# A hybrid decoder block with 15 Strassen pairs instead of 12, eight projection units per head turn, two score buffers, and a softmax division shared by two engines

## The reference, cut to what matters

```python
D_MODEL = 1024; SEQ = 1024; HEAD_DIM = 64; N_Q_HEADS = 16; N_KV_HEADS = 4; WINDOW = BLOCK = 128; CONV_K = 3; D_FF = 2816

proj = jnp.einsum('bsd,de->bse', x, w_in[l])                       # float32, 1024 x 1024 by 1024 x 6656
q, k, v, cb, cc, ch, g_conv, g_attn = jnp.split(proj, SPLIT_POINTS, axis=-1)
y_conv = cb * causal_depthwise_conv(cc * ch, conv_w[l])            # width 3
# sliding-window attention by blocks of 128 queries against their own and the previous 128 keys
scores = where(valid, einsum('bnqkgd,bnskd->bnkgqs', qb, kb) * HEAD_DIM ** -0.5 + alibi, NEG_INF)
m = maximum(max(scores), sink)
p = exp(scores - m)
probs = p / (sum(p) + exp(sink - m))
y_attn = einsum('bnkgqs,bnskd->bnqkgd', probs, vb)
merged = sigmoid(g_conv) * y_conv + sigmoid(g_attn) * y_attn
x = layer_norm(ALPHA * x + einsum('bse,ed->bsd', merged, w_out[l]), ln1_g[l], ln1_b[l])
hid = silu(x @ w_gate[l]) * (x @ w_up[l])
x = layer_norm(ALPHA * x + hid @ w_down[l], ln2_g[l], ln2_b[l])
```

## Time and profile before

| | |
|---|---|
| median of 3 runs | 1359.15 us (1354.24 to 1359.17) |
| the profiled execution's own time | 1358.13 us |
| its span, first to last instruction | 1356.3 us |
| TensorE busy | 1340.0 us, 99% |
| VectorE busy | 848.1 us, 63% |
| ScalarE busy | 528.0 us, 39% |
| GpSimd busy | 724.8 us, 53% |
| mean granted TensorE clock | 0.996 |

### The profile page before, as it was taken

How to read it: one execution, slowest core, us unless ns; L and a number is a source line. 1 busy time by engine, 2 the same in 40 slices (tenths; PEclk the granted TensorE clock), 3 DMA queues, 4 the chain that set the end, 5 groups by cost and what they waited for, 6 DMA issues and landing times. The chain is left out here.

```text
span 1356.3 us, 18062 instructions
## 1 busy us (share of the span) xinstructions
PE 1340.0 (99%) x6506; PEld 1176.5 (87%) x6506; DVE 848.1 (63%) x1167; ACT 528.0 (39%) x973; POOL 724.8 (53%) x487
## 2 busy tenths in 40 slices
PE   9999999999999999999899999999999999999997
PEld 8888888888888888888788888888888888888886
DVE  5665555576867778787968754545546455464547
ACT  6422322336565565755345332232322313223143
POOL 5588788721222121336682775563756637566374
PEclk9999999999999999999999999999999999999999
DMA  6111222121111111112330221211212112111113
GB/s 187 48 55 55 62 63 63 51 59 48 32 34 45 47 32 32 47 48 78 109 93 1 70 71 47 71 54 39 70 46 70 53 40 70 46 59 58 47 55 125
DMA packets 128816, 80.58 MB, mean 59 GB/s; under 512 B 8816, under 2 KB 123504, under 8 KB 128752
## 3 DMA queue, kind: packets, MB, share of 16 engines
q1 hardware_dynamic: 128752, 79.73, 19.8%
HBM read 75.53 MB, written 4.19 MB: 59 GB/s over the span
## 5 line engine op out<-in xcount | busy, mean ns | idle before, releaser
L828 POOL TENSOR_TENSOR w_lo<-raw,w_hi 128x512 fp32r<-128x512 f32 x80 | 110.3, 1379 | 204.0 <-ACT w_hi L1201 204.0
L679 POOL TENSOR_TENSOR w_lo<-raw,w_hi 128x1024 fp32r<-128x1024 f32 x28 | 68.5, 2447 | 219.9 <-ACT w_hi L887 209.9
L1664 DVE TENSOR_TENSOR res<-res,ps 128x512 f32<-128x512 f32 x128 | 87.2, 687 | 59.8 <-PE ps L1835 59.8
L1833 PE MATMUL ps<-hid_hi,wd_hi 128*128 128x512 f32 x320 | 121.5, 380 | 0.1
L1834 PE MATMUL ps<-hid_lo,wd_hi 128*128 128x512 f32 x320 | 121.3, 379 | 0.0
L1835 PE MATMUL ps<-hid_hi,wd_lo 128*128 128x512 f32 x320 | 121.3, 379 | 0.0
L2127 PE MATMUL ps<-act_hi,w_hi 128*128 128x512 f32 x320 | 121.3, 379 | 0.0
L2128 PE MATMUL ps<-act_lo,w_hi 128*128 128x512 f32 x320 | 121.3, 379 | 0.0
L2129 PE MATMUL ps<-act_hi,w_lo 128*128 128x512 f32 x320 | 121.3, 379 | 0.0
L1833 PE MATMUL ps<-act_hi,w_hi 128*128 128x512 f32 x272 | 104.5, 384 | 0.0
L1834 PE MATMUL ps<-act_lo,w_hi 128*128 128x512 f32 x272 | 103.1, 379 | 0.0
(11 more groups left out here) (262 smaller groups left out, 3590.1 us busy)
## 6 DMA issues: line engine op xcount, KB each, us to landing
raw<-in_w_in SPq DMA_DIRECT2D x28, 512.0 KB, 3.8
raw<-in_w_in SPq DMA_DIRECT2D x48, 256.0 KB, 3.0
raw<-in_w_gate SPq DMA_DIRECT2D x40, 256.0 KB, 2.8
raw<-in_w_up SPq DMA_DIRECT2D x40, 256.0 KB, 3.2
raw_d<-in_w_down SPq DMA_DIRECT2D x20, 512.0 KB, 3.4
raw<-in_w_out SPq DMA_DIRECT2D x16, 512.0 KB, 4.0
xs<-in_x SPq DMA_DIRECT2D x8, 512.0 KB, 6.9
out<-rows SPq DMA_DIRECT2D x7, 512.0 KB, 2.7
```

Source lines behind the costliest of these rows:

```text
L828: pool.tensor_tensor(wide(ring(w_lo, n)), src, fp(wide(ring(w_hi, n))), ALU.subtract).then_inc(pl_s, 1)
L1664: dve.tensor_tensor(tile, tile, bank, ALU.add).then_inc(add_s, 1)
L1833: pe.matmul(bank, w_h(t), hi, start=(t == 0), stop=False)
```

## The change

`PLAIN` becomes `(3,)`. Three more (gc, cb) pairs are made ahead of the heads (15 in all), and the turns of the first three heads have 8 units and 8 steps per block; the fourth keeps 12. Consequences in the code:

- The places of the attention's actions in short turns are new. The fourth head's are the same but for the added division.
- There are two score buffers, `sc` and `sc_even`, taken in turn. The exponentials are written back into the same buffer, one column to the left; `exps` is gone. The sink column is written twice per head (prep_dve counts 9 per head instead of 8).
- VectorE multiplies two of the four query heads' probabilities, ScalarE the other two (`divide`, a Copy with the reciprocal as its scale). The transposes wait for both.
- In the fourth turn the ga units are in another order and the weight slots change over (`head_slot`, `before_in_slot`).
- In the first pair GpSimd makes the third weight sum one step earlier. In the output projection's second half the sums x = high + low of token half 1 are spread among the later units instead of standing in one row, and the mean, variance and spread of token half 0 are made earlier on TensorE.

```diff
-PLAIN = (0, 1, 2, 3)
+PLAIN = (3,)
...
-    UNITS += [(_i, 0), (_i + 1, 0), (_i, 1), (_i + 1, 1)]
+    UNITS += [(_i, 0), (_i + 1, 0)] + ([(_i + 1, 1), (_i, 1)] if _k in PLAIN else [(_i, 1), (_i + 1, 1)])
...
-PE_STEPS = sorted([(block_at(b, 0), "scores", b) for b in BLOCKS] + [(block_at(b, 14, 11), "turn", b) for b in BLOCKS]
-                  + [(block_at(b, 20, 15), "values", b) for b in BLOCKS])
+PE_STEPS = sorted([(block_at(b, 0), "scores", b) for b in BLOCKS] + [(block_at(b, 14, 12.5), "turn", b) for b in BLOCKS]
+                  + [(block_at(b, 20, 20.4), "values", b) for b in BLOCKS])
...
+    [(block_at(b, 8.4, 7.7), "divide", b) for b in BLOCKS],
...
-    [(block_at(b, 22.2, 17.2), "values", b) for b in BLOCKS],
+    [(block_at(b, 22.2, 25.5), "values", b) for b in BLOCKS],
...
-    [(LAST_TURN + 113.2 + 0.1 * (m - 6), "mix_second", m) for m in (6, 7)],
+    [(LAST_TURN + 112 + 0.1 * (m - 6), "mix_second", m) for m in (6, 7)],
     [(out_end(DT - 2) + 0.4, "x_second", 0)],
-    [(out_end(DT - 1) + 0.4 + 0.1 * m, "x_second", m) for m in range(1, DT)])
+    [(out_end(DT - 1) + 0.4 + 0.1 * m, "x_second", m) for m in range(1, 3)])
...
-                    act.activation(prob_and_sink(g, lo), sc[:, g, lo:], ACT.Exp, bias=neg_m[:, g:g + 1], scale=-1.0,
+                    act.activation(sc_of(b)[:, g, lo:2 * P + 1], scores_and_sink(b, lo)[:, g], ACT.Exp, bias=neg_m[:, g:g + 1], scale=-1.0,
                                    accum_out=rsum[:, g:g + 1]).then_inc(exp_s, 1)
+
+            def divide(b):
+
+                lo = P if b % NB == 0 else 0
+                act.wait_ge(soft_s, SOFT * b + 3)
+                for g in (2, 3):
+                    act.activation(prob_of(b)[:, g, lo:], prob_of(b)[:, g, lo:], ACT.Copy,
+                                   scale=rden[:, g:g + 1]).then_inc(share_s, 1)
...
-                dve.tensor_tensor(prob[:, :, lo:], prob[:, :, lo:],
-                                  rden[:].rearrange("p (g o) -> p g o", o=1).broadcast_to([P, G, 2 * P - lo]),
+                dve.tensor_tensor(prob_of(b)[:, :2, lo:], prob_of(b)[:, :2, lo:],
+                                  rden[:, :2].rearrange("p (g o) -> p g o", o=1).broadcast_to([P, 2, 2 * P - lo]),
                                   ALU.mult).then_inc(soft_s, 1)
...
                 pe.wait_ge(soft_s, SOFT * b + SOFT)
+                pe.wait_ge(share_s, 2 * b + 2)
...
-                project_out(1, v, {DT + 1: {2: lambda: mean(0)}, DT + 3: {7: lambda: variance(0)},
-                                   DT + 4: {4: lambda: spread(0)}}.get(v, {}))
+                project_out(1, v, {DT: {7: lambda: mean(0)}, DT + 3: {0: lambda: variance(0), 5: lambda: spread(0)}}.get(v, {}))
```

More of the change, by code:

```diff
@@ L140 @@
     [(-40, "weight", 0), (-33, "weight", 1)],
-    [(unit_end(last_unit(t - 2)) + 0.2, "weight", t) for t in range(2, len(HEAD_TILES))],
+    [(unit_end(last_unit(before_in_slot(t))) + 0.2, "weight", t) for t in range(2, len(HEAD_TILES))],
     [(unit_end(last_unit(len(HEAD_TILES) - 2 + v)) + 0.2, "out_weight", v) for v in range(2)],
@@ L144 @@
     [(block_at(b, 4.3), "exp", b) for b in BLOCKS],
-    [(block_at(b, 15.2, 12.1), "turn", b) for b in BLOCKS],
-    [(block_at(b, 21.2, 16.1), "values", b) for b in BLOCKS],
+    [(block_at(b, 8.4, 7.7), "divide", b) for b in BLOCKS],
+    [(block_at(b, 15.2, 13.6), "turn", b) for b in BLOCKS],
+    [(block_at(b, 21.2, 21.5), "values", b) for b in BLOCKS],
     [(-30 if k == 0 else block_at(NB * k - 6, 8.1), "keys", k) for k in range(NKV)],
     [(-31 if k == 0 else block_at(NB * k - 7, 8.1), "value_rows", k) for k in range(NKV)],
-    [(LAST_TURN + 14 + 4 * m, "mix_first", m) for m in range(6)],
+    [(LAST_TURN + 24.3 + 3 * m, "mix_first", m) for m in range(6)],
     [(LAST_TURN + 63.8, "mix_first", m) for m in (6, 7)],
@@ L167 @@
     [(-27 if k == 0 else block_at(NB * k - 1, 8.5, 7.7), "sink", k) for k in range(NKV)],
-    [(LAST_TURN + 14.8 + 4 * m, "mix_first", m) for m in range(6)],
+    [(LAST_TURN + 25.3 + 3 * m, "mix_first", m) for m in range(6)],
     [(LAST_TURN + 64.6, "mix_first", m) for m in (6, 7)],
@@ L1098, in _ @@
                     exponents(n)
+                elif step == "divide":
+                    divide(n)
                 elif step == "turn":
@@ L1586, in _ @@
                     out_sum(n)
-            for v in range(DT, OUT_TILES):
-                if v != OUT_TILES - 2:
-                    out_sum(v)
-                if v == DT + 1:
-                    dve.wait_ge(res_s, DT)
-                    centre(0)
-                if v == DT + 3:
-                    invert(0)
-                if v == DT + 4:
-                    normalise_half(0, range(4))
-                if v == DT + 5:
-                    normalise_half(0, range(4, DT), 6, lambda: out_sum(OUT_TILES - 2))
+            out_sum(DT)
+            dve.wait_ge(res_s, DT)
+            centre(0)
+            x_sum(1, 3)
+            out_sum(DT + 1)
+            x_sum(1, 4)
+            x_sum(1, 5)
+            out_sum(DT + 2)
+            invert(0)
+            x_sum(1, 6)
+            out_sum(DT + 3)
+            normalise_half(0, range(2))
+            x_sum(1, 7)
+            normalise_half(0, range(2, 3))
+            out_sum(DT + 4)
+            normalise_half(0, range(3, 6))
+            out_sum(DT + 5)
+            normalise_half(0, range(6, DT))
+            out_sum(DT + 6)
+            out_sum(DT + 7)
             def hidden_up(h, t):
@@ L1998, in attention_in, with slot @@
             def attention_in(first):
-                return {at - first: (lambda step=step, b=b: attend[step](b)) for at, step, b in PE_STEPS
-                        if first <= at < first + 8}
+                def slot(t):
+                    for at, step, b in PE_STEPS:
+                        if first + t <= at < first + t + 1:
+                            attend[step](b)
+                return {t: (lambda t=t: slot(t)) for t in range(8)}
             for u, (tile, h) in enumerate(UNITS):
```

86 lines of the change are left out of this document (54 added, 32 removed).

## The result

The changed kernel takes 1418.76 us (median of 4 runs, 1416.25 to 1419.21), the kernel before 1358.65 us beside it (4 runs): a ratio of 1.0457, 95% interval 1.0445 to 1.047. It is 4.6% slower. The forecast was 1404 with a range of 1383 to 1421: the side and the main mechanism, the new wait, were right, and 15 us are missing from the sum.

The account below looks back on a forecast made before the run. TensorE, busy 99% of the span, was taken to bound the kernel. 1358.1 - 7.8 (matmuls) + 55.9 (new waits) - 3.2 (tail) = 1403.0 us, given as 1404 for the median; range 1383 to 1421.

Parts of the forecast that it names:

- Part 1: Matmuls on TensorE: three turns lose 288, three extra pairs add 252, so 7.8 us gained.
- the wait of the earlier trace: TensorE's 1.8 us wait for VectorE in the first pair; expected to stay, 0 taken with 2 us either side.
- Part 2: Load of VectorE and ScalarE in short turns: all fits in 62.0 us; score buffers and shared division cost nothing.
- Part 3, the waits: TensorE's values behind VectorE's o_sum in the head turns: 22 new waits, 54.2 us, with slower restarts 55.9.
- Rival 2: Short turns: q's low part delays no softmax, so 34 + 1.6 us instead of 55.9; 1383 us, chance 0.12.
- Part 3, the clock: TensorE after six waits of 3.7 us or more: a lower clock, up to 9 us more, as a bound.
- Rival 3: Turns: the clock falls after long waits, or ScalarE delays exponentials and q copies; 1420 us, chance 0.11.
- Part 4: Tail of the mixer: variance 4.7 and slow matmuls 1.5 go, mean waits 3; 3.2 us gained, bounds 0 and 6.
- the variance's wait: Tail of the mixer, TensorE: the first variance takes 6.5 us; 4.7 us go because it is ready earlier.

Follow-up runs that it names:

- run 1: The changed kernel with q's low part behind softmax and o_sum on VectorE instead of ahead of them: 1378.36 us, 1.0165 of the kernel before.
- run 2: The changed kernel with values 6 or 9 matmuls later in TensorE's order: 1385.84 us, 1.022 of the kernel before.
- run 4: The changed kernel with the tail's mean, variance and spread at their old TensorE places, and VectorE's and ScalarE's old orders behind the turns: 1413.74 us, ratio 1.0434.
- run 3: The changed kernel with twelve pairs and twelve units per turn again, keeping two score buffers, shared division and new tail: 1357.21 us, 1.0009 of the kernel before.
- run 7: The changed kernel with the whole division on VectorE again, nothing on ScalarE: 1419.7 us, 1.0474 of the kernel before.
- run 10: The changed kernel with o_sum ahead of the softmax on VectorE instead of behind it: 1383.35 us, 1.0202 of the kernel before.
- run 6: The changed kernel with the edits of run 1 and run 2, plus old TensorE tail places and two low parts later on VectorE: 1353.0 us, ratio 0.9981.
- run 9: The changed kernel with run 3's twelve units and run 6's tail edit: 1354.7 us, 0.9987 of the kernel before.

## Why the prediction came out as it did

**What bounds.** Right: one wait decides, values behind o_sum, and not load. Runs 1 and 2 take it away from either side of the chain, and the time goes with it.

**Part 1.** The 36 matmuls are gone. Three pairs and the stretch before the turns cost 51.7 us where 3 x 18.1 = 54.4 were reckoned: I had put 0, with 2 to either side, on the third weight sum, and 2.7 came off between the profiled executions. About 2.0 of it is the wait of the earlier trace rows; 0.4 is a first stretch that ends earlier (TensorE goes on there at 12.31 us instead of 12.72, and at 11.54 in run 4, which has the same start as the changed kernel), so it is hardly the change's; and by the medians of run 3 the whole gain may be smaller.

**Part 2.** Right. Run 3 shows it at twelve units, run 7 at eight. ScalarE's division took 0.50 us of the 0.5 assumed, in the changed kernel:

```profile
L1053 ACT ACTIVATE sc<-sc,rden 128x256 f32<-128x256 f32 x32 | 14.4, 502 | 2.1 <-DVE rden L1518 2.1
```

The estimate of 0.49 from the Trainium skill, "ScalarE: Activation LUTs", section "What ACT_TABLE_LOAD costs", agrees with these 502 ns.

**Part 3, the waits.** Right in kind, number and size: 22 waits, 54.2 us forecast, 52.6 measured from start to start. The pattern by blocks, 2.5, 1.99, 1.12, 1.12, 1.99, 3.73, 2.86, 3.81, came as idle times of 2.44, 1.71, 0.85, 0.85, 1.71, 3.44, 2.57, 3.59, 0.2 to 0.3 less each but for the first; 0.16 of that is the counting, since an idle time begins at the modelled end of the matmul before. Rival 2 is refuted by these, and its cause by run 1: q's low part did delay the softmax.

**Part 3, the clock: the step that was too small.** I named it only as a bound ("up to 9 us more", for six waits) and put nothing into the sum, since the one drop in the rows of before came after 6.5 us. It cost 12 us in the turns and 1.5 in the fourth turn's first block, 13.7 in all. It fell behind waits of 3.45, 3.59, 3.44, 3.59 and 2.44 us (at 397.01, 423.03, 482.57, 508.48 and 604.26) and twice more within 1 us behind the end of a wait (580.09, 593.68). Rival 3 had this mechanism and 1420 as its time, nearer to the 1418.76 than the forecast, though its other part, delays on ScalarE, did not come.

**Part 4: the step that failed.** I took the variance's wait away (right, it is gone) and added 3 us for the mean (1.4 came). I did not follow the two other steps that move: the spread, 15 matmuls behind the variance as before, waits 3.5 us for a reciprocal that VectorE now does behind sums of x, and the two m_lo moved ahead lengthen, over GpSimd's channel sum, the wait for the low part of out weights from 0.5 to 1.7. Nor did I price the sums of x: beside GpSimd's work they take up to 2.8 us instead of 0.68, and that, as far as the rows show, is what makes the reciprocal late. The slow matmuls that I took away (1.5) are there again, behind the wait at the spread (nine, about 0.44 us apart, from 739.94 to 743.49). So the tail is 3 us slower, not 3.2 faster. The text spoke of what these steps wait on, but not of what waits on what stands behind them.

**The sum.** Forecast 44.9 us; -2.7 for the first stage, -1.6 for the waits, +13.7 for the clock, +6.1 for the tail make 60.4. That the forecast is only 15 us off is in part luck: 4.3 us too much in two terms stood against 19.8 too little in the two others.

## What to carry over

When work is taken from between two steps of an engine, look for a chain that leaves that engine and comes back in the gap: here the scores, a softmax elsewhere, and an instruction that waits for what stands behind that softmax. The time does not fall below the chain, however idle the other engines are; the cure is the order (run 1: one number, 40 us), either by taking what isn't needed out of the chain, or by putting more of the waiting engine's own work ahead of the wait. Then take the slower clock behind the waits as a term of the sum and not as a margin, follow each moved step's queue one instruction further than the step, and price what stands in that queue from rows with the same neighbour at work (0.68 or 2.8 us for the same sum).

## What was not expected of the hardware

The granted clock fell behind waits much shorter than the 6.5 us of the earlier trace rows: 2.00 us (twice), 2.34 and 2.35 in run 2, 2.04 and 2.05 in run 10, and 2.44 in the changed kernel, while in run 1, where the longest idle time is 1.7 us, it never fell in the turns. It doesn't fall behind every wait of a size: not at 411.33 or 568.04 in the changed kernel, behind 2.58 and 3.44 us, nor at 496.44 in run 10, behind 2.97. In run 4, whose turns have the same waits, it fell in other places (behind the 2.59 us at 407.77, not behind the 3.45 at 396.21), and the three turns together took the same, 247.3 us in both. What else decides is left open.

A sum of two tiles on VectorE took 0.68 us alone and up to 2.85 beside GpSimd's elementwise work. Runs 6 and 9 have the same sum at both lengths, 0.68 and 2.83, with GpSimd's next instruction later or earlier; no run moved GpSimd's work alone.
